# The second block's mixers re-ordered: gate columns inside the attention, an earlier low-rank norm, two branches last in banks of their own

## What is computed

```
proj = x @ w_in                                   # 6856 columns
dq, dk, dv, dz, da, dbeta, glu, c_q, c_kv, k_r, gate_logits = split(proj)
y_dn  = deltanet_branch(dq, dk, dv, dz, da, dbeta, ...)        # ends in @ dn_w_o
y_cv  = conv_branch(glu, ...)      # 31 taps, layer norm, silu, @ w_pw2 + b_pw2
y_mla = mla_branch(c_q, c_kv, k_r, cos, sin, ...)   # rms norm of the low-rank
#   columns, @ w_uq and @ w_ukv, rope, causal attention of 4 heads, @ w_o
gates = sigmoid(gate_logits + b_gate)             # 3 x 1024 columns
merged = gates[0] * y_dn + gates[1] * y_cv + gates[2] * y_mla
return merged @ w_out
```

## Time and the profile before

| | |
|---|---|
| median of 3 runs | 2651.61 us (2647.63 to 2651.77) |
| profiled execution | 2652.34 us, of it span 2650.7 us |
| PE busy | 2506.0 us, 95% |
| DVE, ACT, POOL busy | 62%, 41%, 12% |
| mean granted clock of TensorE | 0.963 of 2.4 GHz |
| first layer's mixer from the end of `proj(17)` to the first transpose after it | 1465.24 to 1666.58 us |
| the same in the second layer | 2237.26 to 2441.45 us |

### The profile page before, as it was taken

How to read it: one execution, slowest core, us unless ns; L and a number is a source line. 1 busy time by engine, 2 the same in 40 slices (tenths; PEclk the granted TensorE clock), 3 DMA queues, 4 the chain that set the end, 5 groups by cost and what they waited for, 6 DMA issues and landing times.

```text
span 2650.7 us, 35863 instructions
## 1 busy us (share of the span) xinstructions
PE 2506.0 (95%) x13317; PEld 2136.8 (81%) x13317; DVE 1633.1 (62%) x1759; ACT 1077.2 (41%) x1219; POOL 325.7 (12%) x429
## 2 busy tenths in 40 slices
PE   7999889999999899999998998999999999998998
PEld 7777857877889788888898986788788888976886
DVE  4897447768875555554567854554645568745545
ACT  2344334444443444444344433344344443433443
POOL 3110111101102000100007200000100026200000
PEclk9999979999999899999999997999999999998999
DMA  7995408958964466556343342556556332533554
GB/s 283 325 330 208 142 22 299 300 200 314 326 211 160 161 222 217 161 185 221 100 128 104 106 151 72 167 190 206 161 190 195 112 90 79 161 112 112 174 185 148
DMA packets 336995, 479.26 MB, mean 181 GB/s; under 512 B 19867, under 2 KB 280314, under 8 KB 336874
## 3 DMA queue, kind: packets, MB, share of 16 engines
q1 hardware_dynamic: 313114, 393.97, 45.5%
q0 software_dynamic: 23760, 83.69, 8.6%
HBM read 476.55 MB, written 1.05 MB: 180 GB/s over the span
## 4 chain that ended last, share of the span: by engine, by line
issue 44%; PE 37%; DVE 9%; DMA 3%; ACT 3%; DVEq 2%; POOL 2%; POOLq 0%; ACTq 0%; SPq 0%
PE ps L903 10%; PE ps L905 10%; PE ps L904 10%; DVE w_lo L1989 3%; DVE diag L2525 2%; DVE mix_mem L2092 1%; DMA probs<-in_w_ada_dram 1%; ACT w_hi L1579 1%; DVEq L2108 1%; PE ps L1160 1%; POOL n_rstd L695 1%; DVEq L2527 1%; DMA spare<-in_w_ada_dram 1%; PE ps L1395 1%; PE ps L968 1%
## 5 line engine op out<-in xcount | busy, mean ns | idle before, releaser
L1989 DVE TENSOR_TENSOR w_lo<-raw,w_hi 128x2048 fp32r<-128x2048 f32 (+1 forms) x368 | 825.5, 2245 | 483.6 <-ACT w_hi L1579 479.8
L1579 ACT ACTIVATE w_hi<-raw 128x2048 fp32r<-128x2048 f32 (+1 forms) x368 | 689.0, 1874 | 384.3 <-PE ps L905 359.0
L903 PE MATMUL ps<-w_hi,x_hi 128*128 128x512 f32 x1424 | 571.1, 401 | 12.5 <-DVE x_lo L2001 7.6
L904 PE MATMUL ps<-w_lo,x_hi 128*128 128x512 f32 x1424 | 559.8, 393 | 0.0
L905 PE MATMUL ps<-w_hi,x_lo 128*128 128x512 f32 x1424 | 559.7, 393 | 0.0
L903 PE MATMUL ps<-x_hi,w_hi 128*128 128x256 f32 (+1 forms) x1152 | 341.0, 296 | 16.5 <-DVE w_lo L1989 13.6
L904 PE MATMUL ps<-x_lo,w_hi 128*128 128x256 f32 (+1 forms) x1152 | 334.0, 290 | 0.0
L905 PE MATMUL ps<-x_hi,w_lo 128*128 128x256 f32 (+1 forms) x1152 | 333.7, 290 | 0.0
L903 PEld LDWEIGHTS ps<-w_hi,x_hi 128*128 128x128 f32 x1424 | 270.6, 190 | 69.7 <-issue 9.9
L905 PEld LDWEIGHTS ps<-w_hi,x_lo 128*128 128x128 f32 x1424 | 270.3, 190 | 58.4
L904 PEld LDWEIGHTS ps<-w_lo,x_hi 128*128 128x128 f32 x1424 | 270.9, 190 | 54.0 <-issue 0.5
(11 more groups left out here) (400 smaller groups left out, 3134.9 us busy)
## 6 DMA issues: line engine op xcount, KB each, us to landing
raw<-in_w_in_dram SPq DMA_DIRECT2D x96, 512.0 KB, 4.6
raw<-in_ffn_w_gate_dram SPq DMA_DIRECT2D x90, 512.0 KB, 4.0
raw<-in_ffn_w_up_dram SPq DMA_DIRECT2D x90, 512.0 KB, 4.9
raw<-in_ffn_wg_dram SPq DMA_DIRECT2D x88, 512.0 KB, 4.7
raw<-in_ffn_wu_dram SPq DMA_DIRECT2D x88, 512.0 KB, 6.0
raw<-in_ffn_wd_dram SPq DMA_DIRECT2D x80, 512.0 KB, 5.0
raw<-in_ffn_w_down_dram SPq DMA_DIRECT2D x80, 512.0 KB, 4.0
spare<-in_w_ada_dram POOLq DMA_DIRECT2D x46, 512.0 KB, 6.3
```

Of the source, the lines that this page charges most:

```text
L903: pe.matmul(dst, wh, vh, start=start, stop=False, skip_group_check=True)
L904: pe.matmul(dst, wh, vl, start=False, stop=False, skip_group_check=True)
L1579: f(w_hi[s][:, 0:n], raw[s][:, 0:n], ACT.Copy).then_inc(hi_ready, 1)
L1989: v.tensor_tensor(w_lo[s][:, 0:n], raw[s][:, 0:n], w_hi[s][:, 0:n].bitcast(F32), ALU.subtract)\
```

## The change

What it does, engine by engine, for each of the two layers:

- **Order of chunks.** The gates of all three branches come before `w_pw2` and `mla_w_o`; `dn_w_o` keeps its place. `uq` and `ukv` are loaded by SyncE, behind a wait for `o_mm` and in front of `dn_w_o`. The layer-norm gains are loaded behind the convolution's `y_lo`.
- **Low-rank norm.** ScalarE squares the low-rank columns before the solver; TensorE sums them after the solver's last products, ahead of `proj(17)`; its rows are made after `o_mm`, and TensorE waits for the scaled columns (`hd_scaled`) after `proj(18)`. VectorE waits for the sums right after the solver, and has four `taps` before `s_state` where it had eight.
- **Small products.** Those with `uq` for the rope stand before `branch(0)`; the others and `ukv` between `proj(21)` and `proj(22)`; the rope and v before `proj(23)`.
- **Convolution.** The sums of its norm are made after `proj(23)`, nine taps stand after the delta-net branch is merged.
- **Attention.** `proj(25)` to `proj(28)` are taken out of the row of projections: group 25 is multiplied into bank 7 after the first three scores (`first`), 26 to 28 in halves of 24 matmuls, one in each of items 0 to 5 (`fill`), in banks 3 and 7. ScalarE adds the bias to them with Identity into `gate_b` and takes one sigmoid over all of it after the attention. Both ScalarE and VectorE get conversions between the items.
- **End.** `branch(1)` (banks 4 to 7) and `branch(2)` (banks 0 to 3) follow the attention directly. `out_rows` uses up each of the first two chunks of `w_out` for both halves of the rows at once.

The diff, cut to its core:

```diff
+
+        gate_b = carve(KT, T)
+
+
+        carve = Carve(16 * P)
         k_nope = carve(HEADS, T)
         v_mla = carve(TT, 512)
-        q_nope = work[:, 4:8, :]
+        q_nope = work[:, 0:4, :]
...
         def pos(g):
 
-            return g if g < 3 else g + 1 if g < 17 else g + 1 + 2 * ((g - 17) // 4)
+            return g if g < 3 else g + 1 if g < 21 else g + 3
...
-                for b, name in enumerate(("dn_w_o_2", "cv_w_pw2_2", "mla_w_o_2")):
+                def gates(b):
                     for j in range(4):
                         load(cols_of(w_in, C_GATE + D * b + 256 * j), KT)
+
+                def branch(name):
                     for j in range(2):
                         load(cols_of(lay(name, l), 512 * j, 512), 4)
 
-                sp.wait_ge(hd_rows, call_h(l, 3) + 1)
+                gates(0)
+
+                sp.wait_ge(o_mm, l + 1)
+                sp.dma_start(uq[:, :, :], a["mla_w_uq_2"][ds(l, 1)].rearrange("o (k p) n -> p (o k) n", p=P))\
+                    .then_inc(mla_w, 16)
+                sp.dma_start(ukv[:, :, :], a["mla_w_ukv_2"][ds(l, 1)].rearrange("o (k p) n -> p (o k) n", p=P))\
+                    .then_inc(mla_w, 16)
+                branch("dn_w_o_2")
+                gates(1)
+                gates(2)
+                branch("cv_w_pw2_2")
+                branch("mla_w_o_2")
+
+                sp.wait_ge(y_lo_ready, call_y(l, 4))
                 ln_gains(l, 1)
...
                     j = TAPS - 1 - sh
+                    if sh == 20:
+                        head_power(call_h(l, 1), 4)
                     if sh == 27:
-                        head_power(call_h(l, 1), 8)
+                        head_power(call_h(l, 2), 8)
...
-                pool.wait_ge(branch_free, l * 2 + 1)
...
-                head_power(call_h(l, 2), 2)
-                head_power(call_h(l, 3), 4)
+                head_power(call_h(l, 3), 2)
...
                 for it in range(ahead_of):
                     scores(it)
+                if first:
+                    first()
                 for it in range(8):
                     turn(it)
                     if it + ahead_of < 8:
                         scores(it + ahead_of)
+                    if fill:
+                        fill(it)
                     values(it)
...
                 last.then_inc(u_mm, 1)
+
+                pe.wait_ge(hd_sq, sq_at(l, 0))
+                for i in range(5):
+                    square = work[:, 4 + i, :] if i < 4 else weights[:]
+                    for t in range(TT):
+                        c = t if i < 3 else 2 + t
+                        last = pe.matmul(ps[:, 3, c:c + 1], square[:, t * P:t * P + P], ones[:, 0:1],
+                                         start=(i == 0 and t == 0), stop=(i in (2, 4)), skip_group_check=True)
+                last.then_inc(hd_stats, 1)
                 proj(17)
                 pe.wait_ge(u_copied, l + 1)
                 for h in range(HEADS):
@@ -1441,24 +1472,57 @@
                     pe.matmul(dst[:, P:T], s_state[:, h, :], q_dec[:, h, :], start=True, stop=False)
                     last = pe.matmul(dst[:, P:T], u_sb[:, 4 + h, :], qk_dec[:, 4 + h, :], start=False, stop=True)
                 last.then_inc(o_mm, 1)
+                head_rows(call_h(l, 1), 4, 3)
                 proj(18)
-                head_sums(4, work, 3, hd_sq, sq_at(l, 0))
+                pe.wait_ge(hd_scaled, l + 2)
+                head_sums(4, work, 3, hd_sq, sq_at(l, 1))
                 proj(19)
-                head_rows(call_h(l, 1), 8, 4)
+                head_rows(call_h(l, 2), 8, 4)
                 proj(20)
 
-                def branch(j, first):
+
+                pe.wait_ge(mla_w, l * 32 + 32)
+                for h in range(HEADS):
+                    for k in range(3):
...
-                branch(0, 0)
+                branch(0, 0, 4, lambda: pe.wait_ge(mla_sb, l * 3 + 1))
                 proj(21)
+                pe.wait_ge(branch_free, l + 1)
+                for h in range(HEADS):
...
+                last.then_inc(mla_mm, 1)
                 proj(22)
-
...
+                pe.wait_ge(mla_sb, l * 3 + 2)
+                for i in range(2):
+                    pe.matmul(ps[:, 4 + i, :], rot[:], q_rope[:, 2 * i:2 * i + 2, :], start=True, stop=True)
+                pe.matmul(ps[:, 3, 0:T], rot[:], k_rope[:], start=True, stop=True).then_inc(rot_mm, 1)
+                ukv_v = ukv[:].rearrange("p k (h n) -> p k h n", h=HEADS)
+                for t in range(TT):
+                    for k in range(2):
+                        last = pe.matmul(ps[:, 6 + t, :], low[:, 3 + k, t * P:t * P + P], ukv_v[:, k, :, P:2 * P],
+                                         start=(k == 0), stop=(k == 1))
+                last.then_inc(mla_mm, 1)
...
+                proj(23)
+                pe.wait_ge(rope_done, l + 1)
+                pe.wait_ge(hd_sq, sq_at(l, 2))
...
                 last.then_inc(hd_stats, 1)
-                proj(23)
-                head_rows(call_h(l, 2), 4, 3)
                 proj(24)
-                pe.wait_ge(branch_free, l * 2 + 1)
-                branch(1, 4)
-
-                pe.wait_ge(hd_sq, sq_at(l, 2))
...
-                pe.wait_ge(evac, evac0 + 29)
+                pe.wait_ge(mla_sb, l * 3 + 3)
+                pe.wait_ge(evac, evac0 + 25)
...
+                def first():
+                    cols_chunk(7, x_hi, x_lo)
+
+                def fill(it):
+
+                    g, m = 26 + it // 2, it % 2
+                    if it < 6:
+                        if it == 0:
+                            pe.wait_ge(cv_scaled, l * 2 + 2)
+                        elif m == 0:
+                            pe.wait_ge(evac, evac0 + (g - 1))
+                        cols_chunk(3 if g % 2 == 0 else 7, x_hi, x_lo, ms=(m,))
+
+                attention(l * 8 + 8, 1, score, v_mla, None, first, fill)
+                pe.wait_ge(evac, evac0 + 29)
+                branch(1, 0, 4)
+                branch(2, 4, 0)
                 def y_pair(i):
                     pe.wait_ge(y_lo_ready, call_y(l, 6) + (i + 1))
 
-                slots = [take(j) for j in range(2)]
                 y_pair(0)
                 for j in range(2):
-                    out_rows(slots[j], (j,), 0, first=j == 0)
-                slots.append(take(2))
+                    s = take()
+                    out_rows(s, (j,), 0, first=j == 0)
+                    used(out_rows(s, (j,), 1, first=j == 0))
+                slots = [take()]
                 y_pair(1)
-                out_rows(slots[2], (2, 3), 0)
-
+                out_rows(slots[0], (2, 3), 0)
+                slots.append(take(1))
                 y_pair(2)
-                for j in range(2):
-                    used(out_rows(slots[j], (j,), 1, first=j == 0))
-                slots.append(take(1))
-                out_rows(slots[3], (4, 5), 0)
+                out_rows(slots[1], (4, 5), 0)
                 slots.append(take(2))
                 y_pair(3)
-                out_rows(slots[4], (6, 7), 0, final=True).then_inc(acc_ready, 1)
-                for j in (2, 3):
-                    used(out_rows(slots[j], (2 * j - 2, 2 * j - 1), 1))
+                out_rows(slots[2], (6, 7), 0, final=True).then_inc(acc_ready, 1)
+                for j in (0, 1):
+                    used(out_rows(slots[j], (2 * j + 2, 2 * j + 3), 1))
                 turn_x(border_b(l, 1), 0, xt)
-                used(out_rows(slots[4], (6, 7), 1, final=True))
+                used(out_rows(slots[2], (6, 7), 1, final=True))
...
-                    if br and j == 0:
-                        act.wait_ge(branch_free, l * 2 + br)
+                    if br == 1 and j == 0:
+                        act.wait_ge(branch_free, l + 1)
+
+                    src = ps[:, 3 if g % 2 == 0 else 7, :] if br == 2 else bank(g)
                     for i in range(2):
                         m = 2 * j + i
-                        last = f(gate[:, m, :], bank(g)[:, T * i:T * i + T], ACT.Sigmoid,
+                        last = f((gate_b if br == 2 else gate)[:, m, :], src[:, T * i:T * i + T],
+                                 ACT.Identity if br == 2 else ACT.Sigmoid,
                                  bias=cols1[:, CB_GATE + 8 * br + m:CB_GATE + 8 * br + m + 1])
                     last.then_inc(evac, 1)
...
                     low_out(g)
+                act.drain()
+                f(work[:, 4:8, :], low[:, 0:4, :], ACT.Square)
+                f(weights[:], low[:, 4, :], ACT.Square).then_inc(hd_sq, 1)
...
                 gate_out(20)
+                act.wait_ge(mla_mm, l * 3 + 1)
+                f(q_rope[:], ps[0:64, 6:8, :].rearrange("p b (k n) -> p (b k) n", k=2), ACT.Copy).then_inc(mla_sb, 1)
                 gate_out(21)
-                ahead(n0 + 27)
+                act.wait_ge(mla_mm, l * 3 + 2)
+                f(q_nope[:], two_banks(4), ACT.Copy)
+                f(k_nope[:], two_banks(6), ACT.Copy).then_inc(mla_sb, 1)
+                gate_out(22)
```

(73 more changed lines are left out.)

143 lines of the change are left out of this document (49 added, 94 removed).

## The result

The changed kernel takes **2615.14 us** (median of 4 runs, 2614.04 to 2616.34). Beside it the kernel before took 2651.11 us (4 runs, 2647.63 to 2651.77). The ratio is 0.9868, with a 95% interval of 0.9852 to 0.9883: 1.3% faster. The profiled execution took 2614.62 us, its span 2613.0 us, against 2652.34 and 2650.7. TensorE is busy 2478.3 us instead of 2506.0 and its mean granted clock is 0.973 instead of 0.963.

A forecast was written before the change was run, and what follows sets the result against it. TensorE bound the kernel, losing 32.7 us a layer in the mixer to standing still and slow clock. With 20.1 left, the layers gain 12.6 and 14.0, together 26.6: 2625 us, 8-in-10 range 2606 to 2645.

The forecast's parts named there:

- rival A: Waits at the scaling and the attention's end vanish with the slow starts behind them: 9.4 us more per layer, 2606; chance 0.13.
- Standing still: From `proj(17)` to the first transpose behind the mixer: TensorE's waits fall from 16.1 to 11.1 us a layer.
- scaled columns: Behind `proj(18)`: TensorE newly waits 2.1 us for `hd_scaled`, since VectorE converts chunk 21 before it scales.
- end of the attention: Items 5 to 7: conversions with no projection left to cover them make TensorE stand still 4.1 us.
- Slow clock: Same part of each layer: time lost to running below full clock falls from 16.6 to 9.0 us.
- charges on sums: Chunks behind one-column sums run slow: 1.5 us each for `proj(17)`, `proj(19)` and the one behind the convolution's sums.
- The second layer: Its mixer is 2.9 us longer at equal standing still; half of that comes back, so it gains 14.0 us.
- item 3: `uq` and `ukv` loaded before `dn_w_o`: TensorE waits at most 0.3 us for the diagonals, 1.8 without the slow chunk before.
- The attention: Attention at granted clock 0.50 before: projections between its items bring 9.0 us a layer back.
- Rival B: Attention: three chunks' conversions each delay TensorE by a `w_lo` of 2.3 us, 6.9 lost per layer, 2639 us; chance 0.20.
- Rival C: Attention: clock stays at 0.50 during the four projections, 19.7 us lost per layer, 2691 us; chance 0.05.
- Rival D: Before `branch(0)`: chunk 22 lands some 13 us later than assumed and the wait eats the gain, 2652 us; chance 0.04.

The follow-up runs named there:

- padded run: Changed kernel with the last four gate chunks ahead of the attention, plus twelve unused matmuls of 256 columns in each of its eight items: 2629.92 us, ratio 0.9928.
- combined run: Changed kernel with last attention split and rounding moved behind it, scaling and diagonals ahead of the solver's split, and the late chunk's rounding earlier: 2593.81 us, ratio 0.9781.
- first experiment: Changed kernel with the last four gate chunks multiplied, rounded and split ahead of the attention instead of between its items: 2627.82 us, ratio 0.9916.

## Why the prediction was right, and where its sizes were off

Forecast: 26.6 us less than before, 2625 us. Measured: 36 us less. Direction, place and mechanism hold; the measured time is inside the range, between the forecast and rival A.

- **Standing still** was forecast to fall from 16.1 to 11.1 a layer; it fell to 10.2. Item by item: `s_state` and `v_new` 0.8 and 1.1 (forecast 0.9 and 0.9); the scaled columns 1.6 (2.1); diagonals none (0.3); `branch_free` 0.2 (0.1); evacuation before the scores none (0.5); end of the attention 2.2 + 1.6 = 3.8 (4.1); `out_rows` one wait of 2.4 (2.1) and the transpose 0.2 (0.1). Following the queues instruction by instruction gave each within 0.5 us.
- **Slow clock** is where the size was off. The forecast left 9.0 of it in place of 16.6, so 7.6 would come back; 11.8 did in the first layer. The terms that were mis-sized are the charges in the solver and behind one-column sums. In the first layer `proj(17)` was charged 1.5 and took 5.82 us at 1.00; `o_mm` 1.3, and its 24 products took 2.8 us, 0.12 each; the chunk behind the convolution's sums 1.5, and it took 5.83 at 1.00. That is 4.3 too much. (In the second layer `o_mm` was slow as charged: 4.41 us, 1.6 more.) The chunk behind the scaling was charged 1.5 and took 8.21 instead of 5.83, with its sums 2.48 instead of 1.70: 3.2. The start of the branches was charged 1.7 and cost 0.9 (24.03 against the padded run's 23.12, and 0.6 more in the last items of the attention, which had no charge), `out_rows` 1.5 as forecast (12.66 against 11.16). The combined run gives a measure for the whole: its 174.27 us busy, less 1.5 for its one slow chunk, is the mixer at full clock, 172.8. The changed kernel has 179.24 there, so 6.4 of slow clock where 9.0 were forecast, and the kernel before 191.09, so 18.3 where I had found 16.6. The two differences, 2.6 and 1.7, are the 4.2 us that the forecast was short. Of the 1.7, 0.9 lie in the attention (below).
- The reasoning behind the charges on sums was that sums of one column make the next chunk slow. The runs say that this is only sometimes so: by the table above, in 5 of 24 layers behind 20 sums and in 8 of 24 behind 32, each time by 1.5 us, but in all 18 layers in which a wait of 1.6 us stood before the sums. So where a wait comes before such sums, the wait is the cause to price.
- **The second layer** was forecast to gain 1.4 us more than the first, half of its extra slow clock; it gained 18.9 against 17.7, 1.2 more. Half was a guess, and it is luck that it came so near.
- **One or the other is paid**, says item 3 of the diagonals' wait (0.3) and the slow chunk 19. The run with only the scaling first bears that out, with 3.3 us at the diagonals where the prediction gave 1.8. The run with the diagonals first shows that neither need be paid.
- **The attention** was the largest term and nearly right: 9.0 forecast to come back. With fills and without the last waits it had 36.01 us of busy time, of which four chunks are 23.3, so its own matmuls take 12.7 at full clock. The kernel before spent 22.63 us on them (row below), 9.9 too many; without fills in the first experiment it was 21.57, 8.9 too many.

```profile
1600.04:1625.14 25.10, 22.63 (x76) 14.63 (x76) 7.31 (x32) 7.33 (x25) 0.00 (x0) 0.57 0.12 42
```

- **Rival A** (all covered, 2606) needed the waits of the scaling and of items 6 and 7 gone. In the changed kernel they are there. The combined run takes both away, and the late chunk's wait in part, and lands at 2593.8.
- **Rival B** (conversions set the pace) is there only at the end: items 0 to 5 show no wait, item 6 shows the 2.2 us of a split.
- **Rival C** (clock stays down): refuted by 24 us at 1.00 among the fills. The Trainium skill ("TensorE: Matmul & The Clock Gate", section "A second HAM failure mode: psum-queue depth-cycling") blames short pauses between groups that change banks; here the fills change banks in every pair of items without a pause, so the rule is not contradicted. The bare attention, with short pauses and a clock of 0.60, is in keeping with it; no run here tells pauses and bank changes apart.
- **Rival D** (late load): it did not happen in this kernel. The load was even earlier than forecast: ScalarE had chunk 22 at 1485.38, 13.8 us after the start of `o_mm` against the 16 assumed, and the run with the load moved back was no faster. It is the next limit, though: with the scaling first, TensorE waited 3.3 us behind it.
- **What the change's parts are worth**, a layer: fills inside the attention 7.5, net all clock; the order of `out_rows` 1.9 by its wait; the branch as a cover 2.1 by its wait. The other 6 to 7 were not tried one by one, so their causes are read from the traces only. Of the 6.2 us of waits for `w_lo` before, 4.6 stood in `out_rows`, where 2.4 are left, and 1.6 ahead of `proj(22)`, which are gone:

```profile
1514.61 0.39 PE L903 MATMUL ps<-x_hi,w_hi 128*128 128x256 f32 x1 [1.55 <-DVE w_lo L1989]
...
1644.85 0.49 PE L903 MATMUL ps<-w_hi,y_hi 128*128 128x512 f32 x1 [1.68 <-DVE w_lo L1989]
...
1653.56 0.50 PE L903 MATMUL ps<-w_hi,y_hi 128*128 128x512 f32 x1 [2.97 <-DVE w_lo L1989]
```

The wait for `s_state` fell from 2.4 to 0.8, and two chunks behind sums that were slow before (1.5 and 1.6 too long) are at full clock, as is `o_mm` in the first layer. Against that stand the new wait for the scaling, 1.6, and 3.2 of slow clock behind it.

## What to carry to other kernels

An engine with strict order and spare time can still set the pace: ask of every conversion what stands behind it, and put it behind whatever the busy engine wants next. Moving five such conversions, without removing any work, gave 21 us on top of the change. A wait on TensorE should be priced with the slow matmuls that may stand behind it: 3.2 us behind the 1.6 of the scaling, 1.5 behind the 3.8 at the attention's end, 1.6 in some layers and nothing in others behind the 2.4 in `out_rows`. Where matmuls are small and broken by pauses, work placed between them is cheap, since the clock gives most of it back: some 11.5 us of padding made the attention 2.65 us longer. When one wait is taken away, look at what stood late behind it: here a load. A forecast should follow the queues for waits, and give the slow clock a range instead of one value for each place.

## What was not expected of the hardware

- 96 matmuls of 256 columns put into the attention lengthened it by 2.65 us and the whole mixer by 0.45, or by 2.1 without what `out_rows` had of its own.
- The slow clock is only partly reproducible in its places. The same chunk with the same neighbours takes 5.8 or 7.3 us, from layer to layer of one execution; the 48 matmuls of `out_rows` behind an unchanged wait of 2.4 us take 11.2 or 12.7. After a wait of 1.2 us they took 11.2 in all four layers, which four layers are too few to tell from chance.
- Small matmuls of 128 columns at 0.12 us each, broken by waits of 0.8 and 1.1 us, kept full clock in the first layer of all twelve profiles, where before they had fallen to 0.63 behind a wait of 2.4 and a shorter one. In the second layer, behind the same waits, they fell to 0.61 in 8 of 12.
- Outside the part that the edits touch, the profiles still differ by up to 6.5 us: the first mixer's solver ended between 1453.0 and 1459.5 us. An edit worth less than about 5 us can't be judged by the median alone; the stretch table of its own part can.
